# A transformer kernel on one core: the first two attention products taken feature tile by feature tile inside the first norm, and the residual loaded in four pieces

## The reference

```
for i in range(DEPTH):
    mod_l = split(silu(c) @ w_mod[i] + b_mod[i], 6)          # from c, one vector
    mod_c = split(silu(c_ctx) @ w_mod[i] + b_mod[i], 6)
    h_l = modulate(rms_norm(x, norm1_g[i]), mod_l[0], mod_l[1])
    h_c = modulate(rms_norm(ctx, norm1_g[i]), mod_c[0], mod_c[1])
    ...
def modulate(h, shift, scale):
    return h * (1 + scale) + shift
```

## Time and profile before

| | |
|---|---|
| median of 3 executions | 3950.46 us (3945.7 to 3951.65) |
| profiled execution: its time | 3946.52 us |
| profiled execution: span, first to last instruction | 3944.7 us |
| PE busy | 3757.0 us (95%), 27404 matmuls |
| DVE busy | 1755.5 us (45%) |
| ACT busy | 1396.6 us (35%) |
| POOL busy | 462.9 us (12%) |
| mean granted clock of TensorE | 0.97 |
| mean DMA rate | 78 GB/s |

### The profile page before, as it was taken

The page is one execution under the profiler, slowest core; times in us unless marked ns, Lnnn a source line. Parts: engine busy times, 40 slices in busy tenths (PEclk is TensorE's granted clock), DMA queues, the critical chain, the costliest instruction groups (busy, mean ns, idle before and its releaser), DMA issues.

```text
span 3944.7 us, 64980 instructions
## 1 busy us (share of the span) xinstructions
PE 3757.0 (95%) x27404; PEld 3355.9 (85%) x27404; DVE 1755.5 (45%) x3158; ACT 1396.6 (35%) x2808; POOL 462.9 (12%) x571
## 2 busy tenths in 40 slices
PE   6999998999998999899999999999997999999998
PEld 5877777888887887788888879999996887999998
DVE  4444465232233455644454463353336545334344
ACT  3444453122123344432322372343233236234232
POOL 1222211000001443100021000010003110011001
PEclk8988989999998999999999999999998999999999
DMA  4022121222233121123221103222221111222222
GB/s 176 33 72 69 53 82 43 97 102 94 96 106 102 60 72 53 65 96 99 94 79 44 49 31 100 86 80 87 92 86 46 46 50 43 94 86 84 92 92 75
DMA packets 88032, 306.07 MB, mean 78 GB/s; under 512 B 9904, under 2 KB 13104, under 8 KB 87616
## 3 DMA queue, kind: packets, MB, share of 16 engines
q1 hardware_dynamic: 84944, 292.72, 21.9%
q0 software_dynamic: 2800, 9.21, 0.7%
HBM read 299.79 MB, written 2.10 MB: 77 GB/s over the span
## 4 chain that ended last, share of the span: by engine, by line
PE 88%; DVE 4%; ACT 4%; DMA 1%; POOL 1%; issue 1%; SPq 0%; DVEq 0%; ACTq 0%; POOLq 0%
PE bank L527 63%; PE bank L589 6%; PE bank L558 2%; PE bank L1008 2%; PE bank L797 2%; PE bank L836 1%; PE bank L681 1%; PE bank L994 1%; PE bank L864 1%; PE bank L742 1%; POOL scratch L2551 1%; PE bank L889 1%; PE bank L876 1%; PE bank L824 1%; PE bank L1130 1%
## 5 line engine op out<-in xcount | busy, mean ns | idle before, releaser
L1772 DVE TENSOR_TENSOR weight_lo<-weight_raw,weight_hi 128x1024 fp32r<-128x1024 f32 (+1 forms) x464 | 560.4, 1211 | 555.3 <-ACT weight_hi L1198 555.2
L527 PE MATMUL bank<-u_hi,weight_hi 128*128 128x256 f32 (+1 forms) x2368 | 685.0, 289 | 8.1 <-DVE u_lo L2491 5.8
L527 PE MATMUL bank<-u_lo,weight_hi 128*128 128x256 f32 (+1 forms) x2368 | 672.4, 284 | 0.0
L527 PE MATMUL bank<-u_hi,weight_lo 128*128 128x256 f32 (+1 forms) x2368 | 671.6, 284 | 0.0
L1198 ACT ACTIVATE weight_hi<-weight_raw 128x1024 fp32r<-128x1024 f32 (+1 forms) x464 | 476.8, 1031 | 526.8 <-PE bank L527 371.0
L527 PE MATMUL bank<-h_hi,weight_hi 128*128 128x512 f32 (+1 forms) x1360 | 500.1, 368 | 18.6 <-DVE h_lo L2193 9.2
L527 PE MATMUL bank<-h_lo,weight_hi 128*128 128x512 f32 (+1 forms) x1360 | 479.6, 353 | 0.0
L527 PE MATMUL bank<-h_hi,weight_lo 128*128 128x512 f32 (+1 forms) x1360 | 479.0, 352 | 0.0
L527 PEld LDWEIGHTS bank<-u_hi,weight_hi 128*128 128x128 f32 x2368 | 448.6, 189 | 34.5 <-issue 28.1
L527 PEld LDWEIGHTS bank<-u_hi,weight_lo 128*128 128x128 f32 x2368 | 448.6, 189 | 0.0
L527 PEld LDWEIGHTS bank<-u_lo,weight_hi 128*128 128x128 f32 x2368 | 447.2, 189 | 0.1
(11 more groups left out here) (272 smaller groups left out, 6954.8 us busy)
## 6 DMA issues: line engine op xcount, KB each, us to landing
weight_raw<-in_w_mlp SPq DMA_DIRECT2D x128, 512.0 KB, 3.5
weight_raw<-in_w_ff SPq DMA_DIRECT2D x128, 512.0 KB, 3.4
weight_raw<-in_w_in SPq DMA_DIRECT2D x92, 512.0 KB, 3.4
weight_raw<-in_w_mod SPq DMA_DIRECT2D x80, 512.0 KB, 3.9
weight_raw<-in_a_w_qkv SPq DMA_DIRECT2D x24, 512.0 KB, 4.3
weight_raw<-in_b_w_qkv SPq DMA_DIRECT2D x24, 512.0 KB, 3.5
first_weight<-in_w_mod SPq DMA_DIRECT2D x16, 512.0 KB, 14.7
weight_raw<-in_w_ret_o SPq DMA_DIRECT2D x16, 512.0 KB, 3.4
```

The costliest lines, as they stand in the source:

```text
L527: m = e.matmul(view[:, 0:hi - lo], a[:, k, :], b[:, k0 + k, lo:hi], start=(k == 0 and i == 0), stop=(k == kt - 1 and i == 2))
L1772: e.tensor_tensor(wlo[s][:, 0:kt, :], raw[n % N_RAW][:, 0:kt, :], whi[s][:, 0:kt, :].bitcast(F32), ALU.subtract).then_inc(*tick("dve_split ...
```

## The change

It has these parts.

1. PE takes the first two products of layer 0 (query and key of head pair 0 of group 0, weights 0 and 1) inside `first_norm`. A new function `products(k)` does feature tile k of both: 12 matmuls, into four PSUM banks that stay open from tile 0 to tile 7. It stands behind `columns_of(k+1)` in the list; `products(7)` comes at the end. `project_heads` skips these two products.
2. `statistics` moves ahead of rows(1); `broadcast` stays behind rows(1).
3. ACT makes the high parts of weights 0 and 1 at k = 1 and of weight 2 at k = 5 (before: all three at k = 3). DVE makes the low parts of weights 0 and 1 at k = 1, behind low(0), and of weight 2 at the end (before: all three at the end).
4. `x` and `ctx` come in four pieces of two feature tiles each (eight DMAs in place of two), and ACT waits for one piece at a time.
5. SP's list: pieces, modulation weights of tile 0, attention weights 0 and 1, modulation weights of tiles 1 to 7, attention weight 2, and then the `axial_table`, which POOL's queue loaded before.

```
--- before.py
+++ after.py
@@ first_norm of tensor_program
+                firsts = [(("qk", 0, 0, 0, kind), weight(("a_w_qkv", KT * kind))) for kind in range(2)]
+                banks = {}
+
+                def products(k):
+                    for job, n in firsts:
+                        h, l = weight_parts(n)
+                        for span, (lo, hi) in enumerate(ALL.spans):
+                            if k == 0:
+                                banks[job, span] = take(*job, span)
+                                e.wait_ge(*at("hi", n))
+                                e.wait_ge(*at("lo", n))
+                            e.wait_ge(*at("hh", norm, k, span))
+                            e.wait_ge(*at("hl", norm, k, span))
+                            for i, (a, b) in enumerate(((h, H_HI), (h, H_LO), (l, H_HI))):
+                                m = e.matmul(banks[job, span][:, 0:hi - lo], a[:, k, :], b[:, k, lo:hi],
+                                             start=(k == 0 and i == 0), stop=(k == KT - 1 and i == 2))
+                            if k == KT - 1:
+                                m.then_inc(*tick("pe_product", ("prod", *job, span)))
+                                done_with[n] = ("prod", *job, span)
+                                close(*job, span)
+
                 view = rows(0)
+                for span in range(2):
+                    statistics(norm, span)
                 for k in range(KT):
                     behind = view
                     if k + 1 < KT:
                         view = rows(k + 1)
                     if k == 0:
                         for span in range(2):
-                            statistics(norm, span)
-                        for span in range(2):
                             broadcast(norm, span)
                     columns_of(k, behind)
+                    if k:
+                        products(k - 1)
                 close("bc", norm, 0)
                 close("bc", norm, 1)
+                products(KT - 1)
@@ project_heads of tensor_program
-                        if (layer, g) != (1, 0) or hh + kind == 2:
+                        if g or hh + kind == 2 or (layer, hh) == (0, 1):
@@ first_norm of scalar_program
-                e.wait_ge(*at("x"))
-                e.wait_ge(*at("ctx"))
                 for k in range(KT):
+                    e.wait_ge(*at("x", k // 2))
...
-                    if k == 3:
-                        split_ahead(0)
+                    if k == 1:
+                        split_up_to(1)
+                    if k == 5:
+                        split_up_to(2)
@@ pool_program
-            e.dma_start(LCL[:, 0:1024], t["con_axial"]).then_inc(*tick("dma_table", ("axial",), by=16))
@@ sync_program
-            e.dma_start(X[:, :, N_META:N_META + N_LAT], t["x"]).then_inc(*tick("dma_x", ("x",), by=16))
-            e.dma_start(X[:, :, N_META + N_LAT:], t["ctx"]).then_inc(*tick("dma_ctx", ("ctx",), by=16))
+            for j in range(KT // 2):
+                k = slice(2 * j, 2 * j + 2)
+                e.dma_start(X[:, k, N_META:N_META + N_LAT], t["x"][:, k, :]).then_inc(*tick(f"dma_x{j}", by=16))
+                e.dma_start(X[:, k, N_META + N_LAT:], t["ctx"][:, k, :]).then_inc(*tick(f"dma_x{j}", ("x", j), by=16))
...
-            first_weights(0, 1, 2, 3)
+            first_weights(0)
             for n, (key, split) in enumerate(order):
+                if n == 2:
+                    first_weights(*range(1, KT))
                 if n == N_RAW:
-                    first_weights(4, 5, 6, 7)
+                    e.dma_start(LCL[:, 0:1024], t["con_axial"]).then_inc(*tick("dma_axial", ("axial",), by=16))
```

## The result

| | before | changed |
|---|---|---|
| median | 3949.57 us (10 executions, 3943.09 to 3951.65) | 3960.55 us (10 executions, 3955.68 to 3969.58) |
| ratio, 95% interval | | 1.0033 [1.0024, 1.0042] |
| span of the profiled execution | 3944.7 us | 3957.3 us |
| first products done and `finish` begins | 73.77 us | 88.91 us |
| from there to the end of the span | 3870.9 us | 3868.4 us |

The account below looks back on a forecast made before the run. PE's chain bounds the kernel, so only the end of the first two products, 73.77 us before, counts. All-low turns +22.1, less 7.7 for the clock, give +14.4 us: 3964.5 us, range 3951 to 3975.

Parts of the forecast that it names:

- The bound: Whole kernel: PE holds 88% of the chain; the effect is the shift of the first two products' end, 73.77 us before.
- Head start: Before the loop: new load order makes columns_of(1) end at 29.5 us in place of 32.88, 3.4 us gained.
- First burst: Start of products(0): waits for low(0) and one weight's low part, so it starts at 33.4 us.
- Turns: Loop in first_norm: PE and DVE alternate without overlap, 9.4 us a turn at the low clock, 6.4 at the high.
- The clock: PE's loop bursts: begin at half rate, rise late; 1.1 us given back on average for 7 turns, 7.7 in all.
- all-low: Loop with PE always at the low clock: 9.4 us a turn, products ending at 95.4 us.
- What the Trainium skill says: Loop bursts: waiting after each K tile throttles PE, so every burst is slow throughout, giving rival B's time.
- rival B: Loop: all bursts at the low clock, +21.6 to +22.1 us, 3972 us; chance 0.14.
- Rival A: Loop pauses: the clock stays high, products end at 75.6 us, +1.8 us, 3952.3; chance 0.20 (up to +7.9).
- Rival C: Loop: DVE and PE overlap after all, products(7) at 55 to 56 us, -18 us, 3932; chance 0.04.
- the wait for the first split at the end is gone, which the sum holds already: End of the old loop: the split wait from 53.18 to 54.61 us disappears, already counted in the sum.

Follow-up runs that it names:

- the version with the turns removed: Changed kernel with PE taking products(k-2) instead of products(k-1) behind columns_of(k): 3934.35 us, ratio 0.9962 to the kernel before.
- The filled pauses: Changed kernel plus 16 discarded 256-column matmuls ahead of products(k-1) from the third feature tile on: 3950.97 us, ratio 1.0007 to the kernel before.
- The edit that makes it true: Changed kernel with only PE's order edited, products(k-2) in place of products(k-1): 3934.35 us, ratio 0.9962 to the kernel before.
- two more steps: Added to products(k-2): tile 1's modulation weights ahead of the attention weights, splits of weights 0 and 1 before the loop: 3932.35 us, ratio 0.9957.

## Why the prediction was right, point by point

- **The bound** was PE's chain, and the shift of one moment. Right: 73.77 became 88.91, +15.1, and the rest of the span differed by -2.5 us (3868.4 against 3870.9), within what that rest varies from kernel to kernel.
- **Head start**, 3.4 us: rows(0) started at 17.05 (16.6 forecast), rows(1) at 22.17 (21.8), `columns_of(1)` ended at 29.2 (29.5). The gain was 3.7 us.
- **First burst** at 33.4: 33.12, released by the first weight's low part, as said.
- **Turns**: pause 2.7 forecast, 2.84 measured; products at the low clock 3.84 forecast, 4.18 measured. The rate was right (0.43 us for 512 columns, 0.21 for 256), but a burst by itself also pays for its start and its end: 0.56 us go by from its first matmul to the second. The others are as in the rows. A turn with rows took 8.79 us on average against "near 8.3".
- **The clock** was forecast mixed, with 1.1 us given back a turn. With the measured pause and burst an all-low turn is 2.84 + 4.18 + 1.87 + 0.96 = 9.85 us and not 9.4, and the turns with rows took 8.79, so they gave back 1.06 on average, as forecast. The last two bursts gave back more: the one at 77.06 us ran high from end to end, and of the last one the second half. The sum was near (end of the products 88.4, forecast "near 88"), but in part by luck: with the measured terms all-low would have ended near 98.4 us and not 95.4, 3 us later, and the clock gave back near 10 us in place of 7.7. The two misses lie in opposite directions.
- **What the Trainium skill says**, in "TensorE: Matmul & The Clock Gate", section "HAM oscillation — how this bites in real kernels" (a wait behind each K tile makes each tile begin cold; do the K tiles in one stretch), agrees with the trace in how bursts begin: six of seven began at 0.50. Taken as the prediction took it, every burst slow from end to end, it is too strong for the time: bursts, rows and columns did not all stay at the low clock, so rival B (+22) overstated the loss by 7. Its cure is right in direction, as the version with the turns removed shows, with one stretch in place of seven.
- **`finish`** waited 0.5 us for ACT, as forecast (88.41 to 88.91).
- **Rival A** priced an always-high clock at +1.8. The filled pauses measured nearly that case: +4.2 at `finish`. Each turn took 6.73 and not 6.4 us (a burst that begins after a wait took 2.35 and not 2.09, and the pause 2.83 and not 2.7), and the first burst, ahead of the filling, still ran low (3.89 us).
- **Rival C** (overlap) was priced at -18, its place named in the two lists. The edit that makes it true gave -15, with two more steps -17. Its price went by DVE's 2.7 us a tile; with the pauses gone PE set the pace, at 3.75 us even at the high clock, so the products ended at 58.6 and not at 55 to 56.
- **What was missed** did not touch this sum but would another. The prediction valued the loads and splits at the head start alone. Against the kernel with loads and splits but no products in the loop, the loop costs 21.6 us of median (3960.55 - 3938.98), not 14: the step "the wait for the first split at the end is gone, which the sum holds already" was true for a loop of turns, but it hid that the moved split alone lets the old order overlap DVE. The change carried its own gain of 10 us and spent it.

## What to carry to other kernels

When a loop makes two engines feed each other, write down one turn of both lists and ask for each wait whether what it asks for stands in front of or behind the other engine's own wait; if behind, the two alternate, whatever their busy time says. In this kernel asking one step later was free and took off 26 us. Before moving work into a loop, look for the single late operand that keeps it out of overlap where it is: here one weight split. And when loads are reordered, every consumer that takes several of them at once is to be moved with them.

## What the runs showed of the hardware

- PE's clock was at 1.00 in the pauses and at 0.50 in the bursts: in the changed kernel 0.53 over 41.4 to 48.5 us, 1.00 over 48.6 to 51.5, 0.51 over 51.5 to 54.9. So a pause of 2.8 us cost its own length and up to 1.85 us more in the burst behind it (4.18 against 2.33).
- The granted clock recorded for a trace's first microseconds does not fit the matmuls there. Before, it stands at 1.00 from 17.93 to 25 us (the earlier trace rows and the window ahead of it), but 32 matmuls of `rows` took 1.94 us at 17.93 and 1.08 at 34.34. The changed kernel's, at 46.09 us and a recorded 0.50, took 1.94 as well.
- A stretch that no edit touches, 3870 us long, varied by 10 us over the ten profiled kernels (3868.4 to 3878.6), and PE's busy time in it from 3706 to 3718 us. Where two of them were compared, in the second attention layer, the longer one had the lower granted clock (0.97 against 0.99). Effects below that need many executions, or the time of a landmark such as `finish`.
